# Two gated output projections by seven quarter products, and the experts' rows turned back by TensorE

## The chip, the cores and the metric

The kernel runs on one core of a Trainium2 chip. The metric is device time in microseconds (us) for one execution, the median of several runs; lower is better. Every matmul here is float32, and one matmul of a 128x128 stationary tile with 512 moving columns shows as two records of the trace.

## What is computed

Two transformer blocks over 512 tokens of 1024 features, in sequence. The first (`first_block`) is a dilated-attention and sparse-attention block with a feed-forward part. The second (`second_block`) has two layers over the 512 tokens and, in its first layer, 256 context rows beside them. Each layer computes, for `x` (and `ctx`):

```
x = x + mod_l[2] * m_l                        # m_l = mix @ w_out, gated by a row of 1024 values
tok = rms_norm(x, norm_ffn) * (1 + mod_l[4]) + mod_l[3]
f = hier_moe(tok)                             # router, then the chosen experts of 16
x = x + mod_l[5] * f
```

Layer 0 does this for 768 rows (six tiles of 128 rows, the last two of them context rows with gates of their own), layer 1 for 512 rows (four tiles). The change concerns `mix @ w_out` with its gate and sum in both layers, and how the rows `tok` are brought into the form in which the experts gather them.

## The kernel before

The program is a list of stages. In each, five engine queues (TensorE `pe`, VectorE `dve`, ScalarE `act`, GpSimd `pool`, SyncE `sp`) run instructions in the order in which they are written and wait on semaphores. At a stage's end `meet` (L3920) has the four compute queues drain and wait for each other; SyncE runs through and only fills weights. Nothing is planned by a scheduler: the order is that of the code.

The output projection of either layer is a `Linear` (L290). Its left operand is `k.HT`, the transposed mix, eight chunks of 128 features; its weights come in four slots of the ring of six. The 1024 output columns go in two blocks of 512, and each tile's block is one PSUM bank filled by eight matmuls: 96 matmuls in layer 0, 64 in layer 1. The first twelve are issued in `begin` (L321), before the stage's boundary; the rest of the first block are L335, the second block, tile by tile, is L364 in `last_block`. VectorE takes each bank by `gated_take` (L3825): one multiplication by the gate from PSUM into a scratch row (L3830), one addition to the tile of `k.X` (L3832), both 128x512.

As soon as a tile has both blocks, `TileNorm` (L823) norms it: ScalarE sums the squares (L853) and takes the root (L855), VectorE takes the reciprocal (L860) and scales the row into `hn` (L862). Two normed tiles are a pair. TensorE transposes a pair by 16 transposes into four PSUM banks (`turn`, L884), VectorE and ScalarE each take two banks into `k.HT` with gain and shift (`take`, L900 and L898). So `k.HT` ends as the transposed `tok`. Pairs but the last are turned between products of the second block; behind the last product come the router's logits of all pairs but the last (`first_logits`, L2500), 9 filler matmuls that keep TensorE busy (`keep_awake`, L1422), and the last pair.

`RowStores` (L2400) is GpSimd's: it loads gain and shift rows by five DMAs (three in layer 1), VectorE makes the gains (L2448), and for each normed tile GpSimd stores `k.X` away (L2435), multiplies `hn` by the gain (L2437, four pieces), adds the shift (L2440, four pieces) and stores the row tile to `moe_rows` (L2442). The experts gather their rows from there.

`Router` (L2461) and `Dispatch` (L2609) follow in the same stage: logits of the last pair, transposes of the logits (L2511), 16 filler matmuls, then a long chain of small VectorE steps with a few TensorE products in it (L2626, L2627, then 28 filler matmuls, L2632, L2636), ending in the lists of rows per expert. GpSimd waits for its row stores, then gathers the first rows (L3081); TensorE transposes them (L2864) and the expert loop starts. SyncE starts the experts' weights when the projection's last weights are used; the load of the fourth expert waits for `places_free`, which TensorE gives after the logits' transposes.

`RowAndTileNorm` (L952) ends the first block. There GpSimd also issues the load of a small rope table (`late`, L1020), just before the stage's boundary. The `OutBySeven` class (L590) already does the first block's own output projection, which has no gate, by seven quarter products.

## Time and profile before

| | |
|---|---|
| median of 3 runs | 2024.25 us (2022.09 to 2025.62) |
| the profiled execution: its time, its span | 2020.34 us, 2018.6 us |
| TensorE busy | 1891.2 us (94%), 10950 matmul records |
| VectorE busy | 1187.0 us (59%) |
| ScalarE, GpSimd busy | 642.7 us (32%), 262.8 us (13%) |
| mean granted TensorE clock | 0.983 |
| layer 0: projection to the first expert product | 1192.8 to 1316.1 us |
| layer 1: projection to the first expert product | 1742.6 to 1836.7 us |

Times in the trace run from the span's start. Busy shares are of the whole span and mix stages in which different engines decide; a stage is read from its timeline, with the idle time before an instruction and what ended it in square brackets.

### The profile page before, as it was taken

The numbers are of one execution on the slowest core, as the hardware profiler recorded it, in microseconds if no ns is written. First come the engines' busy times: TensorE is split into PE (matmuls) and PEld (weight loads), VectorE is DVE, ScalarE is ACT, GpSimd is POOL, SyncE is SP. The second block draws the span as 40 slices with busy tenths as digits, with TensorE's granted clock in tenths as the row PEclk, the third lists the DMA queues.
The fourth block names the chain that finished last, engine by engine and source line by source line (L and its number), as shares of the span: only waits on it lengthen the run. The fifth ranks groups of instructions, "written<-read, shape, count | busy, mean of one in ns | idle before, by whom it ended". The sixth has DMA issues, their size and how long they took to land.

```text
span 2018.6 us, 28998 instructions
## 1 busy us (share of the span) xinstructions
PE 1891.2 (94%) x10950; PEld 1038.5 (51%) x10950; DVE 1187.0 (59%) x1908; ACT 642.7 (32%) x1274; POOL 262.8 (13%) x319
## 2 busy tenths in 40 slices
PE   7999999999999999999998999899997999989993
PEld 4554875544444444555645764633334678645330
DVE  2001777487787653358845644677757667456774
ACT  2011762200000001242313631256643556323551
POOL 3000110011111000012200012611102000051101
PEclk9999999999999999999999999999998989999997
DMA  8632100677666442311111011689965020148995
GB/s 260 169 84 84 54 12 22 219 253 258 235 236 239 147 174 97 133 42 42 42 42 63 1 36 73 266 335 362 363 239 202 1 84 2 35 157 354 387 416 199
DMA packets 108473, 323.89 MB, mean 160 GB/s; under 512 B 9063, under 2 KB 43015, under 8 KB 89904
## 3 DMA queue, kind: packets, MB, share of 16 engines
q1 hardware_dynamic: 77920, 190.56, 26.3%
q0 software_dynamic: 25024, 112.01, 15.6%
q10 hardware_dynamic: 5392, 19.47, 2.4%
q8 instruction: 90, 1.47, 0.3%
q14 instruction: 47, 0.39, 0.1%
HBM read 291.48 MB, written 35.76 MB: 162 GB/s over the span
## 4 chain that ended last, share of the span: by engine, by line
PE 71%; issue 7%; DMA 7%; DVE 6%; PEld 4%; PEldq 2%; ACT 1%; POOL 1%; POOLq 0%; DVEq 0%; SPq 0%; ACTq 0%
PE ps L3441 15%; PE ps L2060 6%; PE ps L466 6%; PE ps L2872 6%; PE ps L1190 5%; PE ps L1236 4%; PE ps L3242 4%; PE ps L1211 4%; DMA X<-moe_rows,row_token 4%; PE ps L364 3%; PE ps L335 2%; PE ps L2893 2%; PE ps L2036 2%; PEld ps L1783 2%; PE ps L1783 1%
## 5 line engine op out<-in xcount | busy, mean ns | idle before, releaser
L3441 PE MATMUL ps<-wide 128*128 128x512 f32 (+1 forms) x736 | 306.5, 575 | 1.9 <-issue 1.7
L3441 PEld LDWEIGHTS ps<-wide 128*128 128x128 f32 x736 | 138.3, 190 | 166.2 <-issue 164.1
L2872 PE MATMUL ps<-wide,X 128*32 x448 | 197.5, 594 | 2.1 <-DVE X L3043 2.1
L2872 PE MATMUL ps<-Z,X 128*32 128x512 f32 x1344 | 197.9, 594 | 0.0
L2060 PE MATMUL ps<-wide 128*128 128x512 f32 (+1 forms) x384 | 148.3, 543 | 0.5 <-issue 0.5
L1544 DVE SCALAR_TENSOR_TENSOR Z<-Z,wide 128x2048 f32<-128x2048 f32 x56 | 131.6, 2349 | 2.8
L1190 PE MATMUL ps<-T 64*128 64x256 f32 (+1 forms) x888 | 109.8, 377 | 8.7 <-DVE nm L1329 6.8
L1783 PE MATMUL ps<-wide 128*128 128x512 f32 x256 | 112.1, 595 | 2.1 <-issue 1.0
L744 ACT ACTIVATE T<-ps 128x512 f32<-128x512 f32 (+2 forms) x139 | 70.7, 536 | 128.2 <-PE ps L1783 109.8
L1261 ACT ACTIVATE T<-T,nm 128x768 f32<-128x768 f32 (+3 forms) x112 | 86.7, 775 | 77.5 <-DVE nm L1329 77.5
L2872 PEld LDWEIGHTS ps<-wide,X 128*32 128x32 f32 x448 | 47.0, 110 | 124.1 <-issue 124.1
L2060 PEld LDWEIGHTS ps<-wide 128*128 128x128 f32 x384 | 71.7, 190 | 68.7 <-issue 65.3
L3476 ACT ACTIVATE Z<-ps 128x512 f32<-128x512 f32 x22 | 13.1, 597 | 289.8 <-PE ps L3441 289.8
L2893 PE MATMUL ps<-T,gw 128*32 x328 | 100.8, 592 | 3.1 <-DVE X L3050 1.4
L746 DVE COPY T<-ps 128x512 f32<-128x512 f32 (+2 forms) x113 | 69.6, 636 | 57.8 <-PE ps L1783 47.8
L1190 PEld LDWEIGHTS ps<-T 64*128 64x128 f32 x888 | 86.3, 192 | 30.2 <-issue 14.0
L1236 PE MATMUL ps<-T,Z 128*64 128x128 f32 x1504 | 98.9, 278 | 0.4 <-ACT wide L1277 0.4
L466 PE MATMUL ps<-wide,T 128*128 128x512 f32 x220 | 94.8, 593 | 0.7 <-DVEq L3922 0.7
L2893 PE MATMUL ps<-X,gw 128*32 128x512 f32 x208 | 93.5, 592 | 0.0
L2893 PE MATMUL ps<-wide,gw 128*32 128x512 f32 x208 | 93.5, 592 | 0.0
L1236 PEld LDWEIGHTS ps<-T,Z 128*64 128x64 f32 x1504 | 80.6, 137 | 13.2 <-issue 13.2
L853 ACT ACTIVATE T<-X 128x1024 f32<-128x1024 f32 x24 | 25.3, 1055 | 192.1 <-DVEq L3833 127.7
(421 smaller groups left out, 3366.0 us busy)
## 6 DMA issues: line engine op xcount, KB each, us to landing
wide<-in_experts SPq DMA_DIRECT2D x64, 1024.0 KB, 9.7
Z<-in_mod_w POOLq DMA_DIRECT2D x32, 1024.0 KB, 5.2
T<-in_experts SPq DMA_DIRECT2D x32, 1024.0 KB, 11.8
X<-in_mod_w POOLq DMA_DIRECT2D x16, 1024.0 KB, 5.3
moe_out<-X ACTq DMA_DIRECT2D x28, 512.0 KB, 8.5
wide<-in_w_down SPq DMA_DIRECT2D x12, 1024.0 KB, 6.8
wide<-in_w_gate SPq DMA_DIRECT2D x22, 512.0 KB, 6.0
wide<-in_w_up SPq DMA_DIRECT2D x22, 512.0 KB, 6.9
```

Source lines behind the costliest of these rows:

```text
L466: last = pe.matmul(self.k.ps[:, self.BANKS[name][i], :], rows[:, c, P * i:P * i + P], weights[:, 512 * x:512 * x + 512], start=(c == 0), s ...
L1190: last = pe.matmul(self.S(i, h)[:, at:at + m], q, keys, start=True, stop=True)
L1211: last = pe.transpose(self.t.bank(c)[:, b * P:(b + 1) * P], src, k.ident[:, :])
L1236: last = pe.matmul(k.ps[64 * h:64 * h + 64, 7, t * P:(t + 1) * P], u["values"][b](h), self.PT[:, j % 2, h, b * P:(b + 1) * P], start=(b * ...
L1261: last = act.activation(p, p, ACT.Exp, scale=-1.0, bias=k.nm[:, pi % 2, c:c + 1], accum_out=k.den[:, pi % 2, c:c + 1])
L1544: ins = dve.scalar_tensor_tensor(acc, w, by, acc, ALU.mult, ALU.add)
L1783: last = pe.matmul(self.banks.bank(u), w, k.HT[:, c, 0:SEQ], start=(c == 0), stop=(c == DK - 1))
L2060: last = pe.matmul(self.lin.bank(u)[:, 0:cn], k.HT[:, c, t * P:(t + 1) * P], w[:, c % 4, :], start=(c == 0), stop=(c == DK - 1))
L2872: last = pe.matmul(ps[rows, t % 2, :], mo.xT[:, c, rows], w_rows, start=(c == 0), stop=(c == DK - 1))
L2893: last = pe.matmul(ps[rows, 5 + hf, :], mo.hidT[:, c, rows], w_rows, start=(c == 0), stop=(c == 1))
L3242: last = pe.matmul(self.banks.bank(u)[:, 0:cn], k.HT[:, c, t * P:(t + 1) * P], w[:, c % 4, :], start=(c == 0), stop=(c == DK - 1))
L3441: last = pe.matmul(self.gu.bank(u)[:, columns], w, self.rhs(c)[:, columns], start=(c == 0), stop=(c == DK - 1))
```

## The change

Both gated projections become `GatedBySeven`: tiles are taken as pairs of an even and an odd row tile (three pairs in layer 0, two in layer 1), features and columns are halved, and each pair's four quarter results come from seven quarter products (P1 to P7, four matmuls each) instead of eight. VectorE makes four sums of rows (S1 to S4) and four of weights (T1 to T4), adds the products together in rows of `k.Z`, multiplies by the gates and adds to `k.X`. ScalarE copies P1 four times over into the two rows of a pair. `begin` now issues P1 of every pair.

GpSimd no longer prepares the experts' rows, and their gain and shift loads go. TensorE turns `k.HT` back (`RowStores.turn`), half a tile at a time in two PSUM banks, ScalarE copies the halves into `k.Z` (`RowStores.copy`) and GpSimd only stores. The first four halves are turned in place of the 9 filler matmuls, the others (eight, or four in layer 1) in place of the 16. The wait for the gate rows moves to VectorE's first gating. The rope table's load moves from GpSimd's queue to ScalarE's.

```diff
+class GatedBySeven(Stage):
+    SUMS = "S1", "S2", "S4", "T1", "T2", "S3", "T3", "T4"
...
+    def begin(self, pe, tiles):
+        self.k.rg.await_landed(pe, self.b11)
+        for i in range(self.n):
+            self.part(pe, "P1", i, self.rows(0, 0), self.b11)
...
+        self.after_sum(pe, "S4")
+        for i in range(n):
+            self.part(pe, "P3", i, self.s4, self.b22)
+        self.after_sum(pe, "T2")
+        for i in range(n):
+            self.part(pe, "P6", i, self.s2, self.t2, 0 if i else 1)
+        for i in range(n):
+            self.part(pe, "P5", i, self.s1, self.t1)
+        self.after_sum(pe, "T4")
+        for i in range(n):
+            self.part(pe, "P7", i, self.s3, self.b12, 0 if i else 1)
+            self.part(pe, "P4", i, self.rows(1, 1), self.b21, 0 if i else 2)
+            if i:
+                self.norm.turn(pe, i - 1)
+        pe.drain().then_inc(k.weights_used, 2)
+        self.between(pe, self.norm)
+        self.norm.tensor(pe)
...
+        for i in range(n):
+            gate = self.gates[:, 0 if 2 * i < ST else 1, :]
+            for row in (0, 1):
+                t = 2 * i + row
+                add(("gated", i, row), self.result(t), gate, ALU.mult)
+                add(("total", i, row), k.X[:, t, :], self.result(t))
+        for i in range(n):
+            gate, x = self.gates[:, 0 if 2 * i < ST else 1, :], k.X[:, 2 * i + 1, :]
+            self.after_part(dve, "P7", i)
+            multiply(("P7", i, "gated"), halves(self.product), twice("P7", i), halves(gate))
+            add(("P7", i, "total"), x, self.product)
+            if i:
+                self.norm.tile(dve, ch, 2 * i - 1)
+            self.after_part(dve, "P4", i)
+            multiply(("P4", i, "gated"), self.product[:, 0:512], self.bank("P4", i), gate[:, 0:512])
+            add(("P4", i, "total"), x[:, 0:512], self.product[:, 0:512])
+            self.norm.tile(dve, ch, 2 * i)
+            if i:
+                self.norm.take(dve, "dve", i - 1)
+        self.norm.tile(dve, ch, 2 * n - 1)
+        self.norm.vector(dve, ch)
...
@@ RowAndTileNorm
+                for dst, src in self.late:
+                    act.dma_start(dst, src).then_inc(k.last_row_stored.sem, 16)
...
-                for dst, src in self.late:
-                    pool.dma_start(dst, src).then_inc(k.small_landed.sem, 16)
...
@@ TileNorm.scalar
+        if self.rows_copies:
+            self.rows_copies(act)
         for p in self.rest:
             self.take(act, "act", p)
...
@@ RowStores
+    FIRST = 4
...
+    def turn(self, pe, a, b):
+        k = self.k
+        for u in range(a, b):
+            t = self.norm.tiles[u // 2]
+            if u >= 2:
+                pe.wait_ge(k.rows_copied.sem, self.copied + u - 1)
+            for j in range(4):
+                last = pe.transpose(self.bank(u)[:, j * P:(j + 1) * P], k.HT[:, 4 * (u % 2) + j, t * P:(t + 1) * P], k.ident[:, :])
+            last.then_inc(k.rows_turned.sem, 1)
...
-            for c in range(0, D, 256):
-                ch.step(pool.tensor_tensor(row[:, c:c + 256], self.norm.hn[:, t, c:c + 256], gain[:, c:c + 256], ALU.mult))
...
+    def store(self, pool):
+        for i, t in enumerate(self.norm.tiles):
+            pool.wait_ge(k.rows_copied.sem, self.copied + 2 * i + 2)
+            pool.dma_start(self.rows_out[t * P:(t + 1) * P, :], self.place(i)).then_inc(k.rows_stored.sem, 16)
...
@@ Router
         self.stores.await_spilled(pool)
+        self.stores.store(pool)
         self.stores.await_rows(pool)
...
         self.logits(pe, 0)
-        keep_awake(pe, k=self.k, bank=norm.banks.first + 3, n=9)
+        self.stores.last_banks_read(pe)
+        self.stores.turn(pe, 0, self.stores.FIRST)
...
         self.banks.filled(last)
+        self.stores.turn(pe, self.stores.FIRST, 2 * len(self.tiles))
         pe.drain().then_inc(k.places_free.sem, 1)
-        keep_awake(pe, k, 7, 16)
```

TensorE's order in layer 0 before, from the last products (L364) with the first pair's transposes (L884) between them, whose only wait is for the normed rows and for a bank:

```order
L364 MATMUL ps<-wide 128x512 [waits weights_landed_1]
L884 MATMUL ps<-ident,T 128x128 [waits norm_rows]
L884 MATMUL ps<-ident,T 128x128 x15
L364 MATMUL ps<-wide 128x512 [waits weights_landed_0,psum_taken_by_vector_0]
L2500 MATMUL ps<-wide,rw 32x512 [waits psum_taken_by_vector_2,psum_taken_by_scalar_2]
L1422 MATMUL ps<-ident 128x128 x9
```

The same place now: L831 are the quarter products (here P7 of pair 1, P4 of pair 1, then P7 of pair 2), L1098 the pair's transposes, L2723 the logits, L2645 the turning back of rows.

```order
L831 MATMUL ps<-wide,Z 128x512 [waits partials_added]
L831 MATMUL ps<-wide,Z 128x512 x3
L831 MATMUL ps<-wide 128x512 [waits partials_added]
L831 MATMUL ps<-wide 128x512 x3
L1098 MATMUL ps<-ident,T 128x128 [waits norm_rows]
L1098 MATMUL ps<-ident,T 128x128 x15
L2723 MATMUL ps<-wide,rw 32x512 [waits psum_taken_by_vector_2,psum_taken_by_scalar_2]
L2645 MATMUL ps<-ident,wide 128x128 [waits partials_added]
L2645 MATMUL ps<-ident,wide 128x128 x7
L2645 MATMUL ps<-ident,wide 128x128 [waits rows_copied]
```

The first pair's transposes still stand between products, in front of the last pair's P7 and P4, and the filler matmuls are gone.

VectorE's order in layer 0 before: a tile is gated (L3830), added (L3832) and normed (L860, L862) before the next tile's product is taken.

```order
L3830 TENSOR_TENSOR T<-ps,T 128x512 [waits vector_order,psum_full_0]
L3832 TENSOR_TENSOR X<-X,T 128x512 [waits vector_order]
L860 RECIPROCAL rstd<-ss 128x1 [waits norm_roots]
L862 TENSOR_SCALAR T<-X,rstd 128x1024 [waits vector_order]
L900 TENSOR_SCALAR wide<-ps,mg,mc 128x256 [waits psum_full_2]
```

Now, from the first gating of tile 0 (L880 are sums and gatings in SBUF, L884 gatings out of PSUM, L1074 and L1076 the norm): the first two rows stand six times in layer 0, once for each tile, before the third.

```order
L880 TENSOR_TENSOR Z<-T,Z 128x1024 [waits partials_added,gate_rows_landed]
L880 TENSOR_TENSOR X<-Z,X 128x1024 [waits partials_added]
L884 TENSOR_TENSOR T<-ps,T 128x1024 [waits partials_added,product_parts_full]
L880 TENSOR_TENSOR X<-T,X 128x1024 [waits partials_added]
L884 TENSOR_TENSOR T<-ps,T 128x512 [waits partials_added,product_parts_full]
L880 TENSOR_TENSOR X<-T,X 128x512 [waits partials_added]
L1074 RECIPROCAL rstd<-ss 128x1 [waits norm_roots]
L1076 TENSOR_SCALAR T<-X,rstd 128x1024 [waits vector_order]
```

All six tiles are gated and added before the first P7 is taken, and the first norm comes behind the first P4.

## Rows read from the trace of the kernel before

**Rows 1.** The page, chain of work that ended last, shares by engine
```profile
PE 71%; issue 7%; DMA 7%; DVE 6%; PEld 4%; PEldq 2%; ACT 1%; POOL 1%; POOLq 0%; DVEq 0%; SPq 0%; ACTq 0%
```
**Rows 2.** Timeline of TensorE, layer 0: start, length, operation, [idle before it and its releaser]
```profile
1203.60 31.14 PE L335 MATMUL ps<-wide 128*128 128x512 f32 x72 [0.23 <-PEq L3922]
...
1257.29 13.90 PE L364 MATMUL ps<-wide 128*128 128x512 f32 x32
1271.03 1.91 PE L884 MATMUL ps<-ident,T 128*128 128x128 f32 x16
...
1280.17 1.93 PE L2500 MATMUL ps<-wide,rw 128*32 128x512 f32 x16 [0.36 <-issue]
...
1284.22 1.97 PE L884 MATMUL ps<-ident,T 128*128 128x128 f32 x16
...
1298.55 6.44 PE L1422 MATMUL ps<-ident 128*128 128x128 f32 x56
1306.16 0.86 PE L2632 MATMUL ps<-Z 128*32 128x128 f32 x24 [1.16 <-DVEq L2693]
```
**Rows 3.** Timeline of VectorE, the first block's projection by seven products
```profile
326.62 1.23 DVE L691 TENSOR_TENSOR T<-wide 128x1024 f32<-128x1024 f32 x1 [5.71 <-PEq L3922]
327.88 1.23 DVE L691 TENSOR_TENSOR T<-T,wide 128x1024 f32<-128x1024 f32 x1
329.13 1.22 DVE L691 TENSOR_TENSOR T<-wide,T 128x1024 f32<-128x1024 f32 x1
330.28 5.20 DVE L700 TENSOR_TENSOR X<-ps,X 128x1024 f32<-128x1024 f32 x4
```
**Rows 4.** Timeline of VectorE, layer 0, second column block
```profile
1248.88 0.69 DVE L3830 TENSOR_TENSOR T<-ps,T 128x512 f32<-128x512 f32 x1 [1.57 <-PE ps L364]
1249.60 2.15 DVE L3832 TENSOR_TENSOR X<-X,T 128x512 f32<-128x512 f32 x1
...
1283.21 0.16 DVE L860 RECIPROCAL rstd<-ss 128x1 f32<-128x1 f32 x1 [1.59 <-ACT ss L855]
1283.41 0.75 DVE L862 TENSOR_SCALAR T<-X,rstd 128x1024 f32<-128x1024 f32 x1
1284.92 1.90 DVE L900 TENSOR_SCALAR wide<-ps,mg,mc 128x256 f32<-128x256 f32 x4 [0.75 <-PE ps L884]
```
**Rows 5.** Timeline of all engines at the boundary ahead of layer 0's input projection
```profile
835.18 0.55 POOL L1020 DMA_DIRECT2D T<-const_rope  x1 [10.66 <-DVE X L996]
...
838.63 1.93 ACT L898 ACTIVATE wide<-ps,mc,mg 128x256 f32<-128x256 f32 x4 [2.24 <-PE ps L884]
...
842.58 1.93 PE L2003 MATMUL ps<-wide 128*32 128x256 f32 x16 [3.11 <-POOLq L3922]
```
**Rows 6.** DMA issues of 834 to 846 us: KB each, median us to landing
```profile
T<-const_rope POOLq DMA_DIRECT2D x1, 256.0 KB, 7.0
```
**Rows 7.** Busy time of PE, PEld, DVE, ACT, POOL; granted clock; DMA share; GB/s
```profile
842.50:846.00 3.50, 3.13 (x18) 1.30 (x19) 1.41 (x2) 1.25 (x3) 0.00 (x0) 0.51 0.11 14
...
1519.30:1528.40 9.10, 0.00 (x0) 0.00 (x0) 4.58 (x5) 1.44 (x3) 7.13 (x8) 0.64 0.96 356
...
1532.00:1535.50 3.50, 3.43 (x4) 1.51 (x5) 2.56 (x3) 0.84 (x1) 0.60 (x1) 0.50 1.02 384
```
**Rows 8.** Timeline of TensorE, layer 1
```profile
1742.56 10.57 PE L321 MATMUL ps<-wide 128*128 128x512 f32 x24
...
1805.01 1.97 PE L884 MATMUL ps<-ident,T 128*128 128x128 f32 x16 [1.12 <-DVE T L862]
...
1818.14 8.10 PE L1422 MATMUL ps<-ident 128*128 128x128 f32 x56
```
**Rows 9.** The page, costliest groups: a ScalarE copy of one bank
```profile
L3476 ACT ACTIVATE Z<-ps 128x512 f32<-128x512 f32 x22 | 13.1, 597 | 289.8 <-PE ps L3441 289.8
```
**Rows 10.** Busy time by stretch, as in rows 7: layer 0 while weights and rows move
```profile
1281.00:1307.50 26.50, 20.34 (x185) 17.54 (x177) 19.27 (x73) 7.28 (x14) 13.03 (x19) 0.94 1.01 403
```
**Rows 11.** Timeline of GpSimd, layer 0: the first gather
```profile
1309.18 1.03 POOL L3081 DMA_INDIRECT X<-moe_rows,row_token  x1 [14.39 <-DVE row_token L2703]
```

More of the change, by code:

```diff
@@ L321, in begin, with last_banks_read @@
                 pe.matmul(self.banks.bank(i)[:, 0:cn], self.lhs(k0 + c, t), w[:, c, :], start=(c == 0), stop=False)
+    def last_banks_read(self, pe):
+        self.banks.taken(pe, len(self.blocks) * len(self.tiles) - 2)
     def tensor(self, pe):
@@ L2422, in place, with bank @@
         return self.k.Z[:, 5120 + D * i:5120 + D * (i + 1)]
+    def bank(self, u):
+        first = (1 if self.n == NT else 5) if u < self.FIRST else 5
+        return self.k.ps[:, first + u % 2, :]
+    def turn(self, pe, a, b):
[7 more added lines that the diff above has]
+            last.then_inc(k.rows_turned.sem, 1)
@@ L2424, in gpsimd, with copy, await_copied @@
+    def copy(self, act, a, b):
+        k = self.k
+        for u in range(a, b):
+            act.wait_ge(k.rows_turned.sem, self.turned + u + 1)
+            act.activation(self.place(u // 2)[:, 512 * (u % 2):512 * (u % 2) + 512], self.bank(u), ACT.Copy).then_inc(k.rows_copied.sem, 1)
+    def await_copied(self, eng, u):
+        eng.wait_ge(self.k.rows_copied.sem, self.copied + u)
     def gpsimd(self, pool, ch):
         k, mo = self.k, self.k.mo
-        for dst, src in self.loads:
-            pool.dma_start(dst, src).then_inc(k.row_mods_landed.sem, 16)
@@ L2428, in gpsimd @@
         for dst, src in ((mo.iota, k.C["iota"]), (mo.token, k.C["token"]), (mo.before, k.C["before"]), (mo.pace, k.C["pace"][:, self.l, :])):
             pool.dma_start(dst, src).then_inc(k.small_landed.sem, 16)
-        pool.wait_ge(k.row_gains_ready.sem, self.ready + len(self.sets))
         for i, t in enumerate(self.norm.tiles):
-            gain, shift = self.sets[0 if t < ST else 1]
-            row = self.place(i)
             pool.wait_ge(k.norm_rows.sem, self.norm.rows + i + 1)
             pool.dma_start(self.away[:, t, :], k.X[:, t, :]).then_inc(k.spilled.sem, 16)
-            for c in range(0, D, 256):
-                ch.step(pool.tensor_tensor(row[:, c:c + 256], self.norm.hn[:, t, c:c + 256], gain[:, c:c + 256], ALU.mult))
-            ch.wait()
-            for c in range(0, D, 256):
-                ch.step(pool.tensor_tensor(row[:, c:c + 256], row[:, c:c + 256], shift[:, c:c + 256], ALU.add))
-            ch.wait()
-            pool.dma_start(self.rows_out[t * P:(t + 1) * P, :], row).then_inc(k.rows_stored.sem, 16)
@@ L2524, in scalar @@
             act.activation(to[:, 0:n, :], x[:, 0:n, :], ACT.Exp).then_inc(k.step_done.sem, 1)
+            if i == 0:
+                self.stores.copy(act, self.stores.FIRST, self.stores.FIRST + 2)
+        self.stores.copy(act, self.stores.FIRST + 2, 2 * n)
     def vector(self, dve, ch):
@@ L3840, in two_blocks, with row_stores @@
         k.expertgate = k.ring[:, 1:3, 1024:SLOT]
-        def row_stores(l, projection, sets):
-            mods = [[bc(scratch["mods"], D, (l * 2 + r) * 6144 + m * D) for m in (3, 4)] for r in range(sets)]
-            projection.row_stores = RowStores(k, l, projection.norm, bc(A["norm_ffn_2"], D, D * l), mods, scratch["h"][l], away)
-            return projection.row_stores
+        def row_stores(l, projection):
+            stores = RowStores(k, l, projection.norm, scratch["h"][l], away)
+            stores.last_banks_read = projection.last_banks_read
+            projection.norm.rows_copies = lambda act: stores.copy(act, 0, stores.FIRST)
+            projection.row_stores = stores
+            return stores
         def moe(l, tiles, head, combine):
@@ L3888, in two_blocks @@
         add(Together(k, Load(k, [(k.X[:, :, :], away)]), even))
-        even.then = Linear(k, hT, DK, A["ev_w_out_2"][0], D, allt, gated_take(k.gatebc), ["dve"] * 12,
-                           norm=mod_sets(0, 1, True))
-        head = [Loading(k, gate_loads(0, 2, 2)), row_stores(0, even.then, 2), even.then]
+        gate_rows = Loading(k, gate_loads(0, 2, 2))
+        even.then = GatedBySeven(k, A["ev_w_out_2"][0], allt, mod_sets(0, 1, True), k.gatebc, gate_rows.landed)
+        head = [gate_rows, row_stores(0, even.then), even.then]
         oddgate = k.Z[:, 9920:9920 + D].unsqueeze(1)
@@ L3916, in two_blocks @@
         add(odd)
-        odd.then = Linear(k, hT, DK, A["od_w_out_2"][0], D, seq, gated_take(oddgate), ["dve"] * 8, norm=mod_sets(1, 1, False))
-        moe(1, seq, [row_stores(1, odd.then, 1), odd.then], lambda y, w: Combine(k, seq, y, out[0], w))
+        odd.then = GatedBySeven(k, A["od_w_out_2"][0], seq, mod_sets(1, 1, False), oddgate)
+        moe(1, seq, [row_stores(1, odd.then), odd.then], lambda y, w: Combine(k, seq, y, out[0], w))
         def meet(eng, i):
```

170 lines of the change are left out of this document (139 added, 31 removed).

## The prediction

> **What bounds the kernel now.** I read the chain of waits first: TensorE holds 71% of it, VectorE 6% [rows 1]. So matmuls taken away are worth their time only where nothing else becomes late. Then the stages that the change touches, each in its timeline. In layer 0's projection TensorE runs its products without a gap: 32 records in 13.74 us from 1257.29 to 1271.03 [rows 2], so 0.429 us a record, 0.858 us a matmul and 3.43 us for a quarter product of four. The last pair is turned at 1284.22 in layer 0 [rows 2] and at 1805.01 in layer 1 [rows 8]; up to these starts I compare, because logits and router follow in the same order. Last the boundary ahead of layer 0's input projection, where TensorE stands idle for 3.11 us and GpSimd's queue ends that [rows 5]. The sum is made against the profiled execution, 2020.34 us, which lies 3.9 us below the median of the three runs, 2024.25; that difference is added at the end. About 0.2%, 4 us, is what a measurement of this kernel can tell from no change.
>
> **The change, part by part.**
>
> *What goes from TensorE.* 96 matmuls become 84 and 64 become 56: 20 x 0.858 = 17.2 us. None of it counts by itself; the end of each stage decides.
>
> *A, the rope load.* GpSimd issues it at 835.18 [rows 5], it lands 7.0 us later [rows 6], so at 842.2, and the boundary opens at 842.58. The next late thing there is ScalarE's last take, 838.63 + 1.93 = 840.56 [rows 5]; with the load on ScalarE's queue I let the boundary open at 841.0: -1.6. After the idle stretch the granted clock is 0.51 over the next 3.5 us [rows 7], that is, the lower of TensorE's two levels, which costs at most half of 3.5 = 1.7; with a shorter stall I take half of it back, -0.8. **A = -2.4.** If the stall vanishes with all of the slow clock: -3.3. If ScalarE's queue has to see the load landed as GpSimd's did: 0 to +0.5.
>
> *B, layer 0's projection.* TensorE begins at 1203.60 [rows 2], P1 being done by then. P2, P3, P6 and P5 of three pairs are 12 x 3.43 = 41.2: 1244.8. VectorE ends its sums of these with two operations of half a row, 0.72 each from start to start [rows 4]: 1246.4 with some lag. Then the order shows twelve operations of 128x1024 (a gating and an addition for each of six tiles) ahead of the first P7. The nearest rows are sums of that shape: they follow at 1.26 and 1.25 us where one waits for the one before, 1.15 where it doesn't, and 5.20 us for four out of PSUM [rows 3]. 12 x 1.26 = 15.1: 1261.5. Pair 0 then takes 1.30 + 1.26 for P7, two times 0.72 for P4, 0.2 + 0.7 for the norm [rows 4], 4.9 in all: 1266.4. Pair 1's P7 (2.56) and the norm of tile 1 (0.9) make the first pair ready to be turned at 1269.9. TensorE had ended P7 and P4 of both pairs (4 x 3.43) at 1258.5: it stands for **11.4 us**, in front of the last pair's P7, which is queued behind the transposes. A stall of 9.1 us in this kernel brought the granted clock to 0.64 in its mean, and it was still 0.50 in a stretch 3.6 us after that [rows 7]. So I let the transposes and P7 run 2 us longer than at full clock: turn (1.91 [rows 2]) to 1271.8, P7 to 1277.2. From there 0.2 + 2.56 + 0.9 for gating, sum and norm, 1.44 for P4, 0.9 for the last norm and 1.9 for the take of pair 1 [rows 4] give 1285.1; logits, 1.93 [rows 2], 1287.0; the turning back of four halves through two banks, with ScalarE's copies at 0.6 us each [rows 9], 2.5 us: the last pair at 1289.5 instead of 1284.22. **B = +5.3.** Without the fall of the clock +3.1; if it falls once more while the last pair is awaited, +7.2.
>
> GpSimd's own work in this stretch costs nothing either way but for its neighbourhood: beside it an addition of 128x512 took 2.15 us where 0.69 is the quiet time of a like operation [rows 4]. That goes away, but it was covered by TensorE's products; only the last tile's, some 0.4 us, lay on the path, and the quiet times above hold it already.
>
> *C, layer 0's router.* Eight halves are turned in place of 16 fillers, paced by ScalarE's copies, 0.6 us each [rows 9], which run beside the router's small steps: +0.5 (0 to 1). Then 28 fillers, 56 records, took 6.44 us at 1298.55 [rows 2], but 8.10 us in layer 1, where the clock was low [rows 8]. With fewer matmuls ahead of them they may be as slow here: +1.66, of which the 1.16 us that TensorE then waits for VectorE [rows 2] hide most: +0.5. **C = +1.0** (0 to 2.2). The gather started at 1309.18, released by the row list [rows 11], while the DMA share was 1.01 of the engines from 1281 to 1307.5 [rows 10]. The row stores, six of 0.5 MB, come later than GpSimd's did; about three more fall into this stretch, 1.6 MB at 403 GB/s = 3.9 us. I have them land between 1311 and 1314, and the row list at about 1314: nothing, but close (a rival below).
>
> *D, layer 1.* P1 is 16 of the 24 records that took 10.57 us from 1742.56 [rows 8], 7.0 us: the stage begins at 1749.7. Eight products, 27.4: 1777.1. Sums 1.7, eight operations of 1.26, pair 0's 4.9, then 2.56 + 0.9: the first pair turned at 1797.2, TensorE having ended at 1790.8, a stall of 6.4 us. All products are behind it there, so that 1.44 + 0.9 + 1.9 follow: 1801.5; logits of one pair, half of 1.93, and four halves 2.5: 1805.0 against 1805.01. At the lower clock up to 3 us more. **D = +0.6.**
>
> *The sum.* -2.4 + 5.3 + 1.0 + 0.6 = **+4.5**: 2024.8 for the profiled execution, and with the 3.9 us up to the median about **2028.8 us**. The 17.2 us of products are bought with VectorE's twelve and eight long operations, which nothing covers.
>
> **A rule weighed.** Rows show a VectorE operation that waits for the one before start 1.26 us after it, and 1.15 us where it needn't [rows 3]. The Trainium skill, "VectorE: DVE Perf Modes", section "The DRAIN you can't avoid", says that a semaphore between VectorE operations costs nothing. The row speaks against it here, by 0.11 us an operation, so it is a rival and not the forecast.
>
> **The rivals.**
>
> 1. *Chained operations as quick as unchained ones* (1.15 us for 1.26). Layer 0 has some 22 long operations between the products' end and the last norm's, 22 x 0.11 = 2.4 us less, layer 1 some 14, 1.5 less: +4.5 - 3.9 = +0.6, so 2024.9. Against it: both steps of 1.26 and 1.25 are of chained operations [rows 3]. 0.08.
>
> 2. *Other side: TensorE's clock outlives the stalls.* If it is full again at once, both behind the 11.4 us stall and at the boundary, A is -3.3, B +3.1, C and D 0: -0.2, 2024.0 us, not slower. It decides at 1270 to 1274 and at 841 to 844: a granted clock near 1.0 there. For it: the transposes of a stall's end are short. Against: 0.51 and 0.50 behind stalls of 3.11 and 9.1 us [rows 5, 7]. 0.17.
>
> 3. *Row stores are late and the gather waits for them.* The last store cannot be issued before ScalarE's last copy, and the queues are full [rows 10]. If two of them land behind the row list, 1 MB at 403 GB/s, 2.6 us, and a store's own way add 3.5 us: 2032.3. 0.20. For it: the share of 1.01. Against: the row list moves later, too.
>
> 4. *VectorE is not the bound.* Were the twelve and eight operations covered, TensorE would end layer 0's six last products at 1244.8 + 20.6 + 1.9 for a turn = 1267, and the last pair could be turned at about 1276, 8 us earlier, in layer 1 6 us earlier: with A about -16, 2008. In-order queue and rows 3 speak against it. 0.08.
>
> That the change leaves the products in place is excluded by its order of instructions.
>
> **How the numbers follow.** Forecast 0.47, rivals 0.08, 0.17, 0.20, 0.08. The bounds of the four terms, not all reached at once, spread the forecast by some 3 us either way around 2028.8, so 0.27 of its 0.47 lie above 2028.3 and 0.20 within 4 us of the old time. Rival 3 gives slower 0.17, same 0.03; rivals 1 and 2 same 0.20, faster 0.04, slower 0.01; rival 4 faster 0.08. Sum: faster 0.12, same 0.43, slower 0.45. The range from 2021 to 2035 takes in rivals 1 to 3 and the forecast with its bounds, but for their tails, and leaves out rival 4.
>
> **What would show it.** Right: in layer 0 the first pair's transposes idle about 11 us, released by the scaling of a normed row on VectorE, in layer 1 about 6 us; VectorE without a gap from 1245 to 1270; granted clock near 0.5 behind 1270; the last pair's transposes some 5 us later than before in layer 0 and at the same time in layer 1; the boundary at about 841 with ScalarE as its releaser; the gather released by the row list. Wrong: the long operations at clearly under 1.2 us; a first pair turned before 1265; the gather released by a DMA; the boundary at 842 or later; a time under 2021 us, which this working cannot give.

## The result, and the profile after

The changed kernel took 2032.43 us in the median of its runs, beside 2022.09 us for the kernel before in the same comparison: ratio 1.0041, 95% interval 1.0025 to 1.0057, that is, 5 to 12 us slower. One of the eight runs of the changed kernel was a slow execution (3790.76 us) and is left out of the ratio. The profiled execution is 13.0 us longer in its span (2031.6 against 2018.6), but 4.3 us of that lie in stretches whose code is the same in both; the table below sorts this out.

TensorE's share of the chain of waits rose from 71% [rows 1] to 76%, VectorE's from 6 to 8%, and the stores of the experts' rows, which had no place in it, now hold 1%:

```profile
PE 76%; DVE 8%; DMA 7%; issue 5%; ACT 2%; PEldq 1%; PEld 1%; POOL 1%; DVEq 0%; ACTq 0%; POOLq 0%; SPq 0%
```

TensorE's timeline in layer 0 (columns as in [rows 2]; L831 are the quarter products, L1098 the transposes of a pair, L2723 logits, L2645 the rows' way back, L1635 fillers):

```profile
1204.60 10.54 PE L831 MATMUL ps<-wide 128*128 128x512 f32 x24 [0.26 <-PEq L4141]
...
1256.17 3.60 PE L831 MATMUL ps<-wide 128*128 128x512 f32 x8
1270.96 3.68 PE L1098 MATMUL ps<-ident,T 128*128 128x128 f32 x16 [11.19 <-DVE T L1076]
1274.43 3.87 PE L831 MATMUL ps<-wide,Z 128*128 128x512 f32 x8
...
1281.74 1.97 PE L1098 MATMUL ps<-ident,T 128*128 128x128 f32 x16
1286.11 1.92 PE L2723 MATMUL ps<-wide,rw 128*32 128x512 f32 x16 [2.40 <-DVE wide L1114]
...
1290.30 1.91 PE L1098 MATMUL ps<-ident,T 128*128 128x128 f32 x16
...
1304.22 6.44 PE L1635 MATMUL ps<-ident 128*128 128x128 f32 x56
...
1323.10 1.97 PE L3091 MATMUL ps<-ident,X 128*128 128x128 f32 x8 [5.66 <-DMA X<-moe_rows,row_token]
1326.12 1.06 PE L3099 MATMUL ps<-wide,X 128*32 x1 [1.05 <-DVE X L3270]
```

The stall of 11.19 us ends with a scaled row of VectorE, as the order of instructions had it. The transposes behind it take 3.68 us where the next ones take 1.97. At the end stands a second stall, 5.66 us for the gathered rows, and behind it matmuls of 1.06 us.

VectorE in that stall: no gap between its operations, the long ones each some 1.25 us behind the last.

```profile
1247.59 1.23 DVE L880 TENSOR_TENSOR Z<-T,Z 128x1024 f32<-128x1024 f32 x1
1248.86 1.23 DVE L880 TENSOR_TENSOR X<-Z,X 128x1024 f32<-128x1024 f32 x1
...
1261.45 1.23 DVE L880 TENSOR_TENSOR X<-Z,X 128x1024 f32<-128x1024 f32 x1
1262.79 1.23 DVE L884 TENSOR_TENSOR T<-ps,T 128x1024 f32<-128x1024 f32 x1
...
1270.15 0.75 DVE L1076 TENSOR_SCALAR T<-X,rstd 128x1024 f32<-128x1024 f32 x1
```

Busy time and granted clock (columns as in [rows 7]; the granted clock, the share of its full speed that TensorE was given, is third from the right) at the boundary, around the two stalls in layer 0, and behind the first pair's stall in layer 1:

```profile
842.40:845.90 3.50, 3.12 (x21) 1.47 (x22) 1.41 (x2) 1.26 (x4) 0.00 (x0) 1.00 0.80 262
...
1271.00:1278.00 7.00, 7.00 (x24) 5.10 (x25) 3.84 (x8) 4.31 (x9) 1.07 (x2) 0.72 0.38 152
...
1290.00:1304.00 14.00, 10.18 (x77) 8.09 (x75) 9.19 (x44) 9.44 (x19) 2.65 (x5) 0.88 1.01 423
...
1323.00:1330.00 7.00, 5.84 (x30) 2.55 (x34) 2.97 (x3) 2.40 (x2) 1.71 (x1) 0.53 0.65 232
...
1808.00:1815.00 7.00, 5.56 (x33) 3.97 (x33) 4.71 (x11) 3.37 (x7) 1.07 (x2) 0.50 0.63 232
```

GpSimd's queue in layer 0 (L2663 stores X away, L2669 stores the experts' rows, L3308 gathers):

```profile
1287.45 0.53 POOL L2663 DMA_DIRECT2D rows_away<-X  x1 [2.57 <-DVE T L1076]
1297.80 1.05 POOL L2669 DMA_DIRECT2D moe_rows<-Z  x2 [9.82 <-DMA rows_away<-X]
...
1304.40 0.53 POOL L2669 DMA_DIRECT2D moe_rows<-Z  x1 [0.81 <-ACT Z L2652]
1318.34 1.03 POOL L3308 DMA_INDIRECT X<-moe_rows,row_token  x1 [13.41 <-DMA moe_rows<-Z]
```

The gather was released by the row list before [rows 11]. Now a store's landing releases it; the last store landed 13.7 us after its issue. The row list was there 4.7 us earlier, at 1313.67 (a cast on VectorE that began at 1313.50 and took 0.17).

Because unchanged stretches differ between executions, the stages are compared by their lengths. *Pair* is the time from the first quarter products (or the first matmuls of the old projection) to the start of the last pair's transposes, in layer 0 from the boundary behind the first twelve matmuls; *list* from there to the transposes that turn the row list; *rows* from there to the transposes of the first gathered rows; *between* from there to layer 1's projection; *end* from layer 1's first gathered rows to the end of the span. All are differences of starts on TensorE's timeline, in us:

| profile of | pair 0 | list 0 | rows 0 | between | pair 1 | list 1 | rows 1 | end |
|---|---|---|---|---|---|---|---|---|
| before | 80.62 | 23.22 | 6.53 | 428.6 | 62.45 | 22.22 | 7.37 | 184.0 |
| after | 85.70 | 22.51 | 10.29 | 430.2 | 64.81 | 21.78 | 8.50 | 183.2 |
| e1_rope | 80.71 | 23.25 | 6.44 | 429.2 | 62.44 | 22.23 | 7.37 | 184.5 |
| e2_products | 106.96 | 26.53 | 6.44 | 431.1 | 73.73 | 25.36 | 7.37 | 182.4 |
| e3_rows | 80.75 | 22.44 | 10.82 | 429.8 | 62.33 | 20.89 | 11.32 | 185.9 |
| e4_order | 84.32 | 22.52 | 6.86 | 428.6 | 63.89 | 20.89 | 9.12 | 183.1 |
| e5_hold | 88.37 | 21.90 | 9.32 | 430.6 | 62.97 | 20.87 | 11.32 | 185.6 |
| e6_unblock | 85.68 | 22.52 | 10.70 | 431.4 | 64.47 | 21.07 | 7.37 | 182.4 |
| e7_rows_early | 80.75 | 22.33 | 11.53 | 431.3 | 62.33 | 22.07 | 8.68 | 183.5 |
| e8_products_gains_later | 92.36 | 27.18 | 6.50 | 429.9 | 65.64 | 26.72 | 7.37 | 183.6 |
| e9_awake | 83.76 | 21.89 | 10.73 | 430.1 | 62.23 | 21.77 | 10.59 | 186.0 |
| e10_late | 85.63 | 22.64 | 6.76 | 428.6 | 63.12 | 21.71 | 7.37 | 190.1 |
| e11_rows_late | 80.75 | 23.04 | 6.53 | 431.6 | 62.33 | 20.96 | 7.37 | 188.8 |
| e12_all | 83.39 | 21.89 | 6.51 | 429.2 | 64.41 | 22.56 | 7.37 | 190.0 |

For the changed kernel against the one before: +5.1, -0.7, +3.8, +1.6, +2.4, -0.4, +1.1, -0.8, in all +12.0. With -3.3 at the boundary (e1, below) that makes **+8.7 us**, inside the measured 5 to 12. The other 4.3 us of the profile's 13.0 are in code that the change does not touch: the stages ahead of 830 us were 1.8 us late, and between 1090 and 1120 us the granted clock was 0.89 in the changed kernel's profile and 1.00 in the other, 2.5 us in its stage.

Each row of the table is one execution, and code that is the same in several rows shows how far that carries. The projections of e5, e6 and e10 are the changed kernel's, with the same stalls of 11.19 and 6.08 us, yet *pair 0* is 85.63 to 85.70 in three of the four profiles and 88.37 in e5, and *pair 1* is 64.81 and 64.47 (e6), but 62.97 and 63.12 (e5, e10). What differs is how long the lower clock lasts behind the stall: over the 7 us behind that of layer 1 the granted clock is 0.50 in the changed kernel's profile and 0.69 in e10's. So a difference of 1 or 2 us between two rows of this table proves little by itself, and +8.7 is as uncertain.

### The profile page after: what moved, and what is told of

Its sections match the earlier page's. It is cut to its first block, busy times and chain, and to the rows that moved or that the text cites. A ratio compares the mean times of both kernels' runs of the same rounds, so it can differ in the third digit from the quotient of the medians.

```text
span 2031.6 us, 28850 instructions
## 1 busy us (share of the span) xinstructions
PE 1884.7 (93%) x10890; PEld 1037.4 (51%) x10890; DVE 1240.9 (61%) x1951; ACT 661.9 (33%) x1299; POOL 195.3 (10%) x230
## 4 chain that ended last, share of the span: by engine, by line
PE 76%; DVE 8%; DMA 7%; issue 5%; ACT 2%; PEldq 1%; PEld 1%; POOL 1%; DVEq 0%; ACTq 0%; POOLq 0%; SPq 0%
PE ps L3668 15%; PE ps L3099 7%; PE ps L469 7%; PE ps L2273 6%; PE ps L1996 6%; PE ps L1403 5%; PE ps L1449 4%; PE ps L1424 4%; PE ps L3469 4%; PE ps L831 4%; PE ps L3120 3%; PE ps L1998 2%; DMA X<-moe_rows,row_token 2%; PE ps L2249 2%; DMA moe_rows<-Z 1%
## 5 line engine op out<-in xcount | busy, mean ns | idle before, releaser
L3668 PE MATMUL ps<-wide 128*128 128x512 f32 (+1 forms) x736 | 306.5, 575 | 1.9 <-issue 1.7
L2273 PE MATMUL ps<-wide 128*128 128x512 f32 (+1 forms) x384 | 148.3, 542 | 0.5 <-issue 0.5
L3469 PE MATMUL ps<-wide 128*128 128x512 f32 (+1 forms) x224 | 79.4, 513 | 1.6 <-issue 1.6
```

Of the source, the lines that this page charges most:

```text
L2273: last = pe.matmul(self.lin.bank(u)[:, 0:cn], k.HT[:, c, t * P:(t + 1) * P], w[:, c % 4, :], start=(c == 0), stop=(c == DK - 1))
L3469: last = pe.matmul(self.banks.bank(u)[:, 0:cn], k.HT[:, c, t * P:(t + 1) * P], w[:, c % 4, :], start=(c == 0), stop=(c == DK - 1))
L3668: last = pe.matmul(self.gu.bank(u)[:, columns], w, self.rhs(c)[:, columns], start=(c == 0), stop=(c == DK - 1))
```

## The experiments

Each ratio is against the kernel before, with its 95% interval; one us is 0.05%.

**e1, the rope load alone** (the kernel before, with the load on ScalarE's queue):

```diff
             if i == ST - 1:
                 act.dma_start(self.away[:, i, :], k.X[:, i, :]).then_inc(k.last_row_stored.sem, 16)
+                for dst, src in self.late:
+                    act.dma_start(dst, src).then_inc(k.last_row_stored.sem, 16)
...
-            if i == ST - 1:
-                for dst, src in self.late:
-                    pool.dma_start(dst, src).then_inc(k.small_landed.sem, 16)
```

> Only the rope table's load moves from GpSimd's queue to ScalarE's. If the boundary ahead of layer 0's input projection waited for GpSimd's queue and that load (theory): idle time there 1.2 us instead of 3.1, ratio to before about 0.999, that is, -1.9 us. If the load is only waited for elsewhere (rival): the boundary at 842.5 as before and no gain.

Measured: 0.9976 (0.9959 to 0.9993), 2019.05 us. The first row is from its TensorE timeline, the second from its table of stretches:

```profile
843.74 1.07 PE L2002 MATMUL ps<-wide 128*32 128x256 f32 x16 [1.18 <-ACTq L3921]
```
```profile
843.60:847.10 3.50, 3.07 (x21) 1.47 (x22) 1.41 (x2) 1.30 (x4) 0.00 (x0) 1.00 0.80 252
```

The idle time is 1.18 instead of 3.11 us and the clock stays at 1.00 where it was 0.51 [rows 5, 7]; from the boundary to layer 0's projection this profile needs 359.65 us, the one before 361.02. Together -1.9 - 1.4 = -3.3 us. The 1.4 is found again in the rows: the 16 matmuls behind the boundary take 1.07 us instead of 1.93, and the 16 records behind them 7.11 instead of 7.70. Of all kernels run this is the only one that is faster than before beyond its interval.

**e2 and e8, the products without the rows' turn.** The changed kernel with GpSimd preparing the rows as before, the fillers back. In e8 VectorE's gain rows moved (this cut is e8 against e2):

```diff
             add(("P2", i), self.result(2 * i)[:, 0:512], self.bank("P2", i))
+        self.row_stores.gains(dve)
         made(self.s3, self.rows(0, 0), self.rows(0, 1))
...
-    def vector(self, dve, ch):
+    def gains(self, dve):
```

> The seven quarter products and the rope load, but the rows are prepared by GpSimd as before, with the filler matmuls back. Theory (VectorE's order of work delays the first pair's transposes, whatever is done with the rows): the stalls of 11 and 6 us ahead of the first pair's transposes stay, last pair in layer 0 some 4 to 6 us later than before; GpSimd gets its first normed row after 1262 and needs about 7 us a tile, so its last store goes out near 1308 and the gather waits for it, as late as in the changed kernel or later: +6 to +12 us on before. Rival (turning the rows back on TensorE is the cost): stalls gone or harmless, +3 us at most.

> The seven quarter products with the rows prepared by GpSimd, as the earlier run, but VectorE makes the gain rows behind P2's sums instead of at the head of its queue, where their loads' landing held the sums S1 to S4 up by 11 and 5 us. Theory: those two stalls are gone, the 11 us stall ahead of the first pair's transposes stays, and GpSimd's rows, begun after 1262 at 7 us a tile, are the late thing: +12 to +22 us on before. Rival (the gains were all that was wrong): as the changed kernel or better, at most +8 us.

Measured: e2 1.0192 (1.0161 to 1.0222), e8 1.0079 (1.0050 to 1.0108). In e2 neither theory nor rival saw the largest part: the gains stood at the head of VectorE's queue and waited for their loads, so that P3, which needs the sum S4, stood for 10.91 us in layer 0, and P3 of layer 1 for 5.22:

```profile
1227.85 33.32 PE L831 MATMUL ps<-wide,T 128*128 128x512 f32 x72 [10.91 <-DVE T L871]
```

In e8 that is gone; its 16 us lie in the range given, but not by the cause given. The gather was released by the row list, not by GpSimd's stores (both rows are of e8's GpSimd):

```profile
1312.21 0.59 POOL L2656 DMA_DIRECT2D moe_rows<-Z  x1 [0.30 <-POOL Z L2654]
1324.44 1.03 POOL L3295 DMA_INDIRECT X<-moe_rows,row_token  x1 [11.63 <-DVE row_token L2917]
```

What is late in the projection is VectorE beside a busy GpSimd. In e8's VectorE timeline, the first and the last of these rows are operations that take 1.23 and 0.75 us in the changed kernel; the one between them, which reads PSUM, keeps its 1.23 us though GpSimd worked beside it from 1278.99 to 1281.77:

```profile
1267.36 3.81 DVE L880 TENSOR_TENSOR X<-T,X 128x1024 f32<-128x1024 f32 x1
...
1279.96 1.23 DVE L884 TENSOR_TENSOR T<-ps,T 128x1024 f32<-128x1024 f32 x1 [2.90 <-PE ps L831]
...
1282.96 3.57 DVE L1077 TENSOR_SCALAR T<-X,rstd 128x1024 f32<-128x1024 f32 x1
```

*pair 0* is 11.7 us longer than before and 6.7 longer than in the changed kernel, and these two operations together are 5.4 longer. *list 0* is 4.0 us longer than before, a part of it because the 56 filler records take 8.95 us at a granted clock of 0.69, instead of 6.44. So with the rows left to GpSimd as in e8, the products cost more (+0.79%) than the whole change does (+0.41%).

**e3, the rows' turn without the products** (the changed kernel with both projections as before, `even.then = Linear(...)`, `odd.then = Linear(...)`).

> The old projection with its eight products, but the rows turned back by TensorE, and the rope load on ScalarE. Theory: no stall ahead of the first pair's transposes, the last pair 1 to 2 us later than before in layer 0 (four halves in place of nine fillers), the gather 2 to 4 us later as the stores go out late; with the rope's -1.9 in all 0 to +3 us on before. Rival (the rows' turn is the whole cost): last pair 5 us later, gather 8 us later, +6 to +8 us. Rival (products are the whole cost): -2 us.

Measured: 1.0021 (1.0002 to 1.0039), above the -0.24% of the rope load by 0.45%, 9 us. Against the kernel before that is +4 us, with an interval of 0 to 8, so the forecast of 0 to +3 is not refuted in its size. Its places were not right: the last pair is not late at all (80.75, 62.33) and the row list is even earlier by 0.8 and 1.3 us, but *rows 0* and *rows 1* are 4.3 and 4.0 us longer, as long as the forecast's upper end or longer. GpSimd's gathers of layers 0 and 1 in e3:

```profile
1308.97 1.04 POOL L3308 DMA_INDIRECT X<-moe_rows,row_token  x1 [14.01 <-DMA moe_rows<-Z]
...
1833.50 1.00 POOL L3308 DMA_INDIRECT X<-moe_rows,row_token  x1 [14.64 <-DMA moe_rows<-Z]
```

So the row stores are late with the rows' turn alone, without the products.

**e4, another order on VectorE**: each pair is gated right before its P7.

```diff
                 add(("total", i, row), k.X[:, t, :], self.result(t))
-        for i in range(n):
-            gate, x = self.gates[:, 0 if 2 * i < ST else 1, :], k.X[:, 2 * i + 1, :]
+            if i:
+                self.norm.tile(dve, ch, 2 * i - 1)
+            x = k.X[:, 2 * i + 1, :]
             self.after_part(dve, "P7", i)
...
             add(("P7", i, "total"), x, self.product)
-            if i:
-                self.norm.tile(dve, ch, 2 * i - 1)
```

> The changed kernel with one order changed on VectorE: each pair's gating and sums stand right before that pair's P7, not all pairs' ahead of the first, and the norm of a pair's second tile behind the next pair's gating. Same instructions, same number. Theory (the order is the cost): first pair turned near 1262 instead of 1271 in layer 0, stall under 4 us, last pair 4 to 6 us earlier, layer 1 2 to 3 us earlier: 6 to 9 us less than the changed kernel, so -1 to +2 us on before. Rival (VectorE's amount of work is the cost): the last pair no more than 1 us earlier, time as the changed kernel's.

Measured: 1.0008 (0.9990 to 1.0026), 0.33% or 6.7 us less than the changed kernel. The first pair is turned 58.8 us after the start instead of 66.4, and the stall is 3.63 us:

```profile
1259.26 3.57 PE L1098 MATMUL ps<-ident,T 128*128 128x128 f32 x16 [3.63 <-DVE T L1076]
...
1271.62 2.56 PE L1098 MATMUL ps<-ident,T 128*128 128x128 f32 x16 [1.92 <-DVE T L1076]
1278.41 3.64 PE L2723 MATMUL ps<-wide,rw 128*32 128x512 f32 x16 [4.22 <-DVE wide L1114]
```

But the last pair came only 1.4 us earlier in layer 0 and 0.9 in layer 1: there the rival was nearer. VectorE is now what everything waits for, the logits too (4.22 us). Its timeline in e4 shows no idle time from the first of these rows to the last, 35.6 us:

```profile
1243.45 1.23 DVE L881 TENSOR_TENSOR Z<-T,Z 128x1024 f32<-128x1024 f32 x1
...
1278.26 0.75 DVE L1076 TENSOR_SCALAR T<-X,rstd 128x1024 f32<-128x1024 f32 x1
```

So of the 5.1 us this order takes back 1.4, and 3.7 stay. Not all of these are VectorE's work: behind the wait of 4.22 us the logits take 3.64 us, where they took 1.92 in the changed kernel. And between 1217 and 1242 VectorE stood idle for 12.8 us in all, waiting for products, since its queue has the sums of all pairs ahead of the first gating. An order that gates a pair as soon as its own sums are made, with TensorE's products pair by pair, might use that time and was not tried. The rest of the gain is in *rows 0* (-3.4), *between* (-1.6) and *list 1* (-0.9). The reason for the first, as the traces have it and not tested by itself: TensorE ends its products 8 us earlier, the experts' weights, issued behind them, start 5.4 us earlier (73.8 instead of 79.2 us after the projection's start), and the stores issued behind these land 10.1 us after issue instead of 13.7.

**e5 and e10, the fourth expert's loads** (2 MB on SyncE). e5 issues them behind the landing of the row stores, e10 behind the first gathers and five matrices of the first experts:

```diff
             if e == PLACES - 1:
                 sp.wait_ge(k.places_free.sem, self.freed + 1)
+                self.router.stores.await_rows(sp)
             self.load_gate_up(sp, e)
-        self.router.stores.await_rows(sp)
```
```diff
-        for e in range(PLACES):
-            if e == PLACES - 1:
-                sp.wait_ge(k.places_free.sem, self.freed + 1)
+        for e in range(PLACES - 1):
             self.load_gate_up(sp, e)
+        sp.wait_ge(k.places_free.sem, self.freed + 1)
...
         for e in range(DOWNS):
             self.load_down(sp, e)
+        self.load_gate_up(sp, PLACES - 1)
```

> The changed kernel, but SyncE issues the fourth expert's two loads (2 MB) behind the landing of the row stores instead of ahead of it. Theory (the row stores' bytes share the DMA engines with the experts' weights, and land late by that): the gather starts 3 to 4 us earlier in layer 0 and 2 to 3 us earlier in layer 1, released by the row list; 4 to 7 us less than the changed kernel, +1 to +4 us on before. Rival (the stores are late by when they are issued, or by the way of a single store): gather as late as before this edit, no gain.

> The changed kernel, but the fourth expert's two loads (2 MB) go behind the first gathers and the experts' third matrices, not ahead of the row stores' landing (and not beside the gather, as in the run that only held them for the stores). Theory (bytes ahead of the gathered rows set the start of the experts): gather 3 to 4 us earlier in layer 0, released by the row list, and landed in 4.8 us; first transposes of the experts 3 to 4 us earlier in layer 0, 1 us in layer 1 where 60 records of fillers end just before; 3 to 5 us less than the changed kernel, +3 to +5 us on before. Rival (the store's and gather's own way, whatever else is moved): no gain.

Measured: e5 1.0063 (1.0040 to 1.0085), e10 1.0035 (1.0019 to 1.0051). In e5 the first half of the theory came true and the gain did not. These are GpSimd's gather, and TensorE's wait for what it brings, in e5:

```profile
1315.04 1.04 POOL L3308 DMA_INDIRECT X<-moe_rows,row_token  x1 [9.59 <-DVE row_token L2930]
```
```profile
1322.65 1.40 PE L3091 MATMUL ps<-ident,X 128*128 128x128 f32 x8 [4.69 <-DMA X<-moe_rows,row_token]
```

The row list releases the gather, but its rows take 7.6 us to arrive (changed kernel: 1318.34 to 1323.10, 4.8 us), since the 2 MB that were held back now move beside them. In e10 they move behind, and both halves hold:

```profile
1316.94 1.03 POOL L3308 DMA_INDIRECT X<-moe_rows,row_token  x1 [9.68 <-DVE row_token L2930]
```
```profile
1321.99 1.09 PE L3091 MATMUL ps<-ident,X 128*128 128x128 f32 x8 [2.12 <-DMA X<-moe_rows,row_token]
```

*rows 0* is back at 6.76 us and *between* at 428.6. In e11 and e12, which have the same edit, *rows 0* is 6.53 and 6.51. That the bytes ahead of the gathered rows make them late in layer 0 is thereby shown. But the time is the changed kernel's, because layer 1 pays: the experts' weights are themselves late there, as the longest wait of ScalarE for them shows (waits in the last 180 us: us in total, times, longest), first in the changed kernel, then in e10, and *end* is 6.9 us longer.

```profile
ACT Z L3167 <- DMA wide<-in_experts: 12.5, 3, 5.0
```
```profile
ACT Z L3167 <- DMA wide<-in_experts: 20.2, 6, 10.0
```

**e6, the row stores ahead of the wait for X's stores**:

```diff
+        self.stores.store(pool)
         self.stores.await_spilled(pool)
...
-        self.stores.store(pool)
```

> The changed kernel, but GpSimd issues the row stores ahead of its wait for the landed rows of X, which stood before them and ended last there (9.8 and 8.4 us). Theory (bytes against the experts' weights): the first two stores go out some 8 us earlier, the last still behind ScalarE's last copy at 1304; gather 0 to 1.5 us earlier in layer 0, 0 to 1 us in layer 1: 0 to 2.5 us less than the changed kernel. Rival (the wait for the spilled rows is what makes the stores late): gather released by the row list, 4 to 7 us less.

Measured: 1.0029 (1.0013 to 1.0045). *rows 0* stayed at 10.70, *rows 1* went back to 7.37 in this one profile; the difference to the changed kernel, 2.4 us, is within both intervals. The wait of 9.82 us in GpSimd's queue, which the prediction had overlooked, is not what makes layer 0's rows late.

**e7, e11, e12, combinations.** e7 is e3 with the edits of e5 and e6, e11 is e3 with those of e6 and e10, e12 is e4 with those of e6 and e10.

> The old products with the rows turned back by TensorE (as the earlier run), with both edits of the row stores: issued ahead of the wait, and the fourth expert's loads behind them. The row list there was 0.65 us earlier than before in layer 0 and 1.5 us earlier in layer 1, counted from the projection's start. Theory: the gather follows the row list, so layer 0 ends 0 to 1 us and layer 1 0.5 to 1.5 us earlier than before, and with the rope's 2 to 5 us the ratio to before is 0.997 to 0.9985. Rival (turning back costs elsewhere): no better than +2 us.

> The old products with the rows turned back by TensorE and the rope load on ScalarE, the row stores issued ahead of the wait for the spilled rows, and the fourth expert's loads behind the gathers. Theory: gather released by the row list, which is 0.65 us and 1.5 us earlier than before; with the rope's gain 2.5 to 5 us less than before, ratio 0.9975 to 0.999, below every kernel so far but the rope's alone. Rival (the rows' way by TensorE costs wherever the loads stand): +3 us as the two earlier runs of this kind.

> All of the change with its repairs: each pair gated right before its P7, row stores ahead of the wait for the spilled rows, the fourth expert's loads behind the gathers. Theory: VectorE's amount of work still has the last pair 3 to 4 us late in layer 0 and 1 to 1.5 us in layer 1, the gather then follows the row list: -1 to +1.5 us on before, 1 to 2 us less than the run with the new order alone; the products cannot win. Rival (only order and late stores were wrong): -4 us or more, since 20 matmuls are saved.

Measured: e7 1.0017 (1.0002 to 1.0033), e11 1.0006 (0.9991 to 1.0021), e12 1.0023 (1.0004 to 1.0041). e7 missed for e5's reason (*rows 0* 11.5 us); in e11 and e12 the gathers follow the row list in both layers, and the 5 to 6 us come back at the end (188.8 and 190.0), as in e10. All three measured slower than forecast (e12 with its forecast still inside its interval), and none beats the rope load alone. e12 and e11 differ by the products alone (with e4's order), both with their rows in time: 1.0023 against 1.0006, with intervals that overlap, so there too the 20 saved matmuls bring nothing that can be measured. The fourth expert's loads late in layer 0 alone were not tried.

**e9, fillers in the stall**, so that TensorE works ahead of the first pair's transposes:

```diff
             if i:
+                if i == 1:
+                    keep_awake(pe, k, self.norm.banks.first + 3, 44 if n == 3 else 22)
                 self.norm.turn(pe, i - 1)
```

> The changed kernel with filler matmuls on TensorE ahead of the first pair's transposes: 44 in layer 0 (10 us), 22 in layer 1 (5 us), so that it works through its stalls. Theory (the stalls cost 2 us and 1.8 us more through the clock that is low behind them): granted clock near 1.0 there, transposes 1.9 us instead of 3.7, P7 3.4; last pair 2 us earlier in layer 0 and 1.5 in layer 1; the gather follows by 0 to 2 us, as the row stores are the late thing: 1 to 3.5 us less than the changed kernel. Rival (the clock plays no part): no difference, or slower by the fillers' overhang.

Measured: 1.0048 (1.0029 to 1.0067), no gain in all. In the projection the theory holds: the last pair is 1.9 us earlier than in the changed kernel in layer 0 (2.0 forecast) and 2.6 in layer 1 (1.5 forecast; against the profiles of e5 and e10 it is 0.7 and 0.9), the transposes take 1.97 us, and the clock stays at 1.00. The rows are of e9's timeline and stretches:

```profile
1255.61 9.99 PE L1637 MATMUL ps<-ident 128*128 128x128 f32 x88
1266.96 1.97 PE L1100 MATMUL ps<-ident,T 128*128 128x128 f32 x16 [1.37 <-DVE T L1078]
```
```profile
1268.00:1276.00 8.00, 7.99 (x27) 3.82 (x26) 6.31 (x12) 4.60 (x10) 0.53 (x1) 1.00 0.32 131
```

It is given back where the rows are late: *rows 1* +2.1 and *end* +2.8; of the latter, 3.0 us are the first expert tile of layer 1, which takes 12.10 us instead of 9.14, at a granted clock of 0.64 instead of 1.00 over its first 7 us.

## Why the prediction was right or wrong

The time, 2032.4 us, lay in the range and on the forecast side. The forecast itself, 2028.8, was 3.6 us below it, and the sum, +4.5, was about half of the +8.7 that the profiles give by terms: -3.3, +5.1, +4.7 and +2.2. The layer 0 projection was foreseen; that the range held the rest is owed to its width and to rival 3, whose 2032.3 is nearest.

- **A, forecast -2.4, shown -3.3 (e1).** Place, mechanism and releaser were right (ScalarE's queue ends the idle time). The clock did not fall at all, where I had taken half of its loss as saved; so the number of the bound came, though 1.18 us of the stall stay. The boundary opened at 842.49, which I had named as a sign of being wrong: the stages ahead of it were 1.8 us late in that profile, so a fixed time within the execution was no fit sign.
- **B, forecast +5.3, measured +5.1.** Each step came out: the first pair at 66.4 us after the start (66.3 forecast), a stall of 11.19 us (11.4), 2 us of slow clock behind it (3.68 - 1.91 and 3.87 - 3.60; e9 removes 1.9), operations at 1.25 us. That it came so close is in part luck: the same code needed 2.7 us more in e5. The queue in front of the last pair's P7, which I had stressed, is the smaller part: with that order mended (e4), 3.7 of the 5.1 us stay, while VectorE works without a gap.
- **C, forecast +1.0, measured -0.7 + 3.8 + 1.6.** The failed step is "I have them land between 1311 and 1314": the last store landed at 1318, so a DMA released the gather, the other named sign of being wrong. The stores stand behind X's stores (which e6 takes away without gain in layer 0), behind ScalarE's copies, and among the experts' weights (e10 takes 2 MB of these away, and the delay goes); rival 3 (0.20) gave +3.5 for that, and +3.8 came. The slower fillers did not come (6.44 us again), and the eight halves cost nothing on the path. Missing altogether was what the late rows do next: TensorE stands for 5.66 us, and the granted clock is 0.53 in the 7 us of the first expert tile behind that. The tile takes 11.7 us (1323.10 to 1334.82) where it took 9.15 before (1313.97 to 1323.12); net, +1.6 is left in *between*. All six profiles with late rows have such a tile (11.5 to 13.0 us). Of the eight with rows in time, before, e1, e4, e10 and e12 have 9.1 to 9.2 us, but e2, e8 and e11 have 10.7, 10.8 and 11.9. So late rows bring the slow tile, and it can come without them: what else decides stays open.
- **D, forecast +0.6, measured +2.4 - 0.4 + 1.1 - 0.8 = +2.2.** The stall was 6.08 us (6.4), but the clock fell to 0.50 behind it; the step that failed here is the size of that. The working had come out at 1805.0 against 1805.01; the +0.6 was set between that and a bound of 3 us, without a row for it. But it is a step of this one profile: e5 and e10, with the same projection and the same stall, have *pair 1* +0.5 and +0.7 longer than before, as forecast. How long the lower clock lasts behind a stall is what the prediction could not fix. The +1.1 is layer 1's gather, which waits for the row stores there as well; the prediction had no term for it.
- **Rival 1.** The changed kernel's long operations follow each other by 1.25 us, each waiting for the one before: it fell with its condition. No run has these operations without the wait, so what the waiting itself costs is not shown.
- **Rivals 2 and 4.** The clock at the boundary did outlive its stall, those at 1271 and 1808 did not. VectorE covered nothing.

Which half loses more cannot be told from these runs, because the two overlap. The rows' turn alone costs 9 us (e3 against e1), and the products on top of it 4 more (1.0041 against 1.0021, with intervals that overlap). In the changed kernel's own terms, though, the two projections make +7.4 of the +12.0 and all that follows them +4.6. The prediction had +5.3 and +0.6 for the projections and +1.0 for the turn in layer 0.

## What to carry to other kernels

Work that leaves TensorE for an engine that stands behind it in the same stage is saved only as far as that engine has gaps: sum the receiver's queue from the first product that it needs to the last, before counting matmuls. When a store is moved later, list all bytes that are then in flight up to the first reader, and give the list's time as a bound; holding back other loads only helps if they do not meet the read itself, and if no later stage lives on them. Where TensorE waits for data, price the slow clock of the stage behind the wait as well.

## What the runs showed of the hardware that was not expected

- A stall of 1.18 us left the granted clock at 1.00 (e1, changed kernel), 3.11 us brought 0.51 [rows 5, 7]; behind 5.66 us the granted clock in the first expert tile was 0.53 and the tile was 2.6 us longer. The length of the stall did not decide alone: ahead of the same tile 1.90 us before left it at 9.15 us, 1.91 us in e11 gave 0.62 over 7 us and 11.9 us.
- Beside a working GpSimd a VectorE addition of 128x1024 in SBUF took 3.81 us instead of 1.23, 3.1 times as long, as with the 2.15 against 0.69 us of [rows 4]; a scaling of 128x1024 took 3.57 instead of 0.75, 4.8 times as long (e8). Multiplications that read PSUM kept their 1.23 and 0.68 us in the same stretch.
- Code that no edit touched varied by several us between executions: with the rope load moved, the boundary (at 842.58 us before) lay between 840.09 (e3) and 845.92 us (e12), and the way from there to layer 0's projection took about 359.6 us in six of these profiles and 362.0 in the other seven.
